# Half-precision pairs of the expert weights, split during projection and recurrent stage, and the experts' products as three passes

## What is computed

```python
def hier_moe(x, ...):                       # x: (tokens, 1024)
    grp  = argmax(xf @ router_coarse_w + b)          # 1 of 4 groups
    top_v, top_i = top_k(fine logits of that group, 2)   # 2 of 4 experts in it
    gate = softmax(top_v) * softmax(coarse)[grp]
    h = silu(xf @ expert_w1[e]) * (xf @ expert_w3[e])     # 1024 -> 256, 16 experts
    y = sum over the two experts of gate * (h @ expert_w2[e])   # 256 -> 1024
```

## Time and profile before

| | us |
|---|---|
| median of 3 runs | 1721.48 |
| profiled execution, its own time | 1725.69 |
| span of that execution, first to last instruction | 1724.1 |
| TensorE busy in the span | 1496.3 (87%) |
| VectorE, ScalarE, GpSimd busy | 796.5, 391.0, 358.0 |

### The profile page before, as it was taken

The page is one execution under the profiler, slowest core; times in us unless marked ns, Lnnn a source line. Parts: engine busy times, 40 slices in busy tenths (PEclk is TensorE's granted clock), DMA queues, the critical chain, the costliest instruction groups (busy, mean ns, idle before and its releaser), DMA issues. The chain is left out here.

```text
span 1724.1 us, 23759 instructions
## 1 busy us (share of the span) xinstructions
PE 1496.3 (87%) x8642; PEld 963.1 (56%) x8643; DVE 796.5 (46%) x1363; ACT 391.0 (23%) x689; POOL 358.0 (21%) x328
## 2 busy tenths in 40 slices
PE   6999999699898998998889399706999999995987
PEld 3555566388787787887776155503444444442443
DVE  5333111357766767677676644430111111124775
ACT  3001111123223222233221222101222222221332
POOL 0000000043352441533522111131000000002321
PEclk9999999899999999999988599857999999997999
DMA  9755442501012020120101522198577664314331
GB/s 390 264 203 184 178 149 112 206 1 66 13 66 80 1 78 29 51 78 13 36 13 57 199 110 109 55 356 320 206 301 294 249 233 176 109 67 150 131 126 54
DMA packets 60789, 237.74 MB, mean 138 GB/s; under 512 B 6672, under 2 KB 23696, under 8 KB 53912
## 3 DMA queue, kind: packets, MB, share of 16 engines
q1 hardware_dynamic: 37912, 152.30, 23.6%
q0 software_dynamic: 18176, 67.38, 10.5%
q10 hardware_dynamic: 4608, 16.78, 2.4%
HBM read 153.85 MB, written 82.61 MB: 137 GB/s over the span
## 5 line engine op out<-in xcount | busy, mean ns | idle before, releaser
L2065 PE MATMUL ex_ps<-ex_w,ex_xT 128*128 x512 | 227.3, 597 | 1.5 <-issue 1.5
L292 PE MATMUL pj_ps<-pj_wh,pj_xh 128*128 128x448 f16 (+1 forms) x576 | 196.1, 340 | 14.5 <-DVE pj_wl L181 14.5
L292 PE MATMUL pj_ps<-pj_wl,pj_xh 128*128 128x448 f16 (+1 forms) x576 | 196.2, 341 | 0.0
L292 PE MATMUL pj_ps<-pj_wh,pj_xl 128*128 128x448 f16 (+1 forms) x576 | 196.0, 340 | 0.0
L2065 PEld LDWEIGHTS ex_ps<-ex_w,ex_xT 128*128 128x128 f32 x512 | 95.6, 192 | 110.5 <-issue 110.5
L1491 POOL TENSOR_TENSOR mx_ET<-mx_G,arena 128x512 f32<-128x512 f32 x80 | 117.1, 1484 | 145.9 <-ACT mx_G L1040 136.5
L2168 DVE SCALAR_TENSOR_TENSOR ex_th<-ex_th,ex_ps 128x256 f32<-128x256 f32 x32 | 13.5, 421 | 233.1 <-ACT ex_th L2126 233.1
L2080 PE MATMUL ex_ps<-arena,ex_hidT 128*128 x256 | 115.3, 593 | 0.7 <-ACT ex_hidT L2130 0.7
L789 PE MATMUL mx_ps<-mx_M,mx_ET 128*128 128x128 f32 x672 | 94.1, 295 | 20.2 <-POOL mx_ET L1491 19.1
L804 PE MATMUL mx_ps<-mx_X,mx_MT 128*128 128x128 f32 x656 | 94.6, 290 | 11.3 <-ACT mx_X L1048 11.3
L789 PEld LDWEIGHTS mx_ps<-mx_M,mx_ET 128*128 128x128 f32 x672 | 85.2, 205 | 34.3 <-POOL mx_ET L1491 22.5
(11 more groups left out here) (415 smaller groups left out, 2593.0 us busy)
## 6 DMA issues: line engine op xcount, KB each, us to landing
ex_w<-in_w SPq DMA_DIRECT2D x16, 2048.0 KB, 9.0
sorted_h<-pj_zero POOLq DMA_DIRECT2D x32, 512.0 KB, 3.2
arena<-in_w SPq DMA_DIRECT2D x16, 1024.0 KB, 11.9
ex_x<-sorted_h POOLq DMA_DIRECT2D x32, 512.0 KB, 9.6
sorted_y<-ex_y ACTq DMA_DIRECT2D x32, 512.0 KB, 2.8
proj<-arena SPq DMA_DIRECT2D x72, 224.0 KB
pj_w<-in_w_mixed SPq DMA_DIRECT2D x4, 1792.0 KB, 14.0
mx_past<-proj SPq DMA_DIRECT2D x8, 896.0 KB, 6.6
```

Of the source, the lines that this page charges most:

```text
L292: mm = nc.tensor.matmul(bank[b][:, 0:width], x[:, m, k], packed(y, u, mixed)[:, k], start=(k == 0 and n == 0), stop=(k == KD - 1 and n == 2))
L2065: m = mm(B[u][:], xT[u][:, k], w13[:, slot, k].rearrange("p one f -> p (one f)"), start=(k == 0), stop=(k == KD - 1))
```

## The change

The experts' weights (16 x 3 MB) are handed to the program as 96 pieces of 128 x 1024 (`wx`), six per expert. Each piece is loaded, split into a high and a low half-precision part (scaled by 64, as in `project`), and written to a DRAM tensor `ws` in pairs. Pieces 0 to 60 are split in `project`, one per step from step 8 on, through a ring of four in the space of x (GpSimd issues load and store); pieces 61 to 95 in `mixer`, five per tile in tiles 0 to 6, through two slots in the space of `s0T` and `r0` (ScalarE issues load and store). So `s0T` and `r0` are loaded later, after the last pair is out. The zero fill moves from GpSimd in `project` to SP at the start of `mixer`, with rows of 1 KB. In `experts` the weights are loaded as pairs (the same bytes), x and the hidden rows are split after their transposes, and each product is three half-precision passes. The scales are taken back in the tanh, in the hidden split and in the routing weights.

```diff
@@ project: GpSimd, in place of the zero fill
+                def store(c):
+                    pool.wait_ge(pair_lo, c + 1)
+                    pool.dma_start(ws[c], pair[c % ring]).then_inc(pair_out[c % ring], 16)
+                pool.wait_ge(x_lo, 3)
+                for c in range(EARLY_CHUNKS):
+                    if c >= ring:
+                        pool.wait_ge(pair_out[c % ring], 16 * (c // ring))
+                    pool.dma_start(raw[c % ring], wx[c]).then_inc(raw_in[c % ring], 16)
+                    if c >= 2:
+                        store(c - 2)
...
@@ project: ScalarE and VectorE, at the end of each step
+                        act.wait_ge(raw_in[c % ring], 16 * (c // ring + 1))
+                        split_hi(nc.scalar, pair[c % ring][:, 0], raw[c % ring], W_SCALE).then_inc(pair_hi, 1)
...
+                        dve.wait_ge(pair_hi, c + 1)
+                        split_lo(nc.vector, pair[c % ring][:, 1], raw[c % ring], W_SCALE, pair[c % ring][:, 0]).then_inc(pair_lo, 1)
@@ mixer: SP
-            sp.dma_start(s0T[:], s0T_d).then_inc(s0T_in.sem, 16)
-            sp.dma_start(r0[:], r0_d).then_inc(s0T_in.sem, 16)
             load(1, 1, 0)
+            sp.wait_ge(half_set.sem, 3)
+            for j in range(SLOTS // P):
+                sp.dma_start(sorted_h.rearrange("(j p) (b c) -> j p b c", p=P, b=4)[j], zero[:].unsqueeze(1).broadcast_to([P, 4, 256])).then_inc(zeroed.sem, 16)
...
             load(NT, 0, NT // 2, sample=True)
+            for n in range(2):
+                sp.wait_ge(pair_out[n].sem, 16 * ((TILE_CHUNKS * (NT - 1) - n + 1) // 2))
+            sp.dma_start(s0T[:], s0T_d).then_inc(s0T_in.sem, 16)
+            sp.dma_start(r0[:], r0_d).then_inc(s0T_in.sem, 16)
             store(NT - 2)
@@ mixer: ScalarE
+            def put(t, u, m):
+                act.wait_ge(pair_d.sem, pair_d.at(t, m + 1))
+                at = (u + m) % 2
+                act.dma_start(ws[EARLY_CHUNKS + TILE_CHUNKS * t + m], pair[at]).then_inc(pair_out[at].sem, 16)
+            def chunk(t, u, i, m):
...
+                if m > 0:
+                    put(t, u, m - 1)
+                elif later(t, 1):
+                    put(t - 1, 1 - u, TILE_CHUNKS - 1)
+                if m < TILE_CHUNKS - 1:
+                    fetch(t, u, m + 1)
+                at, earlier = (u + m) % 2, TILE_CHUNKS * i + (TILE_CHUNKS * u + m) // 2
+                if later(t, 1) or m >= 2:
+                    act.wait_ge(pair_out[at].sem, 16 * earlier)
+                act.wait_ge(raw_in[at].sem, 16 * (earlier + 1))
+                split_hi(nc.scalar, pair[at][:, 0], raw[at], W_SCALE).then_inc(pair_a.sem, 1)
...
             def body(t, u, i):
                 turn(t)
+                first_fetch(t, u)
...
                 level(t, 1)
+                chunk(t, u, i, 0)
                 level(t, 2)
+                chunk(t, u, i, 1)
                 level(t, 3)
                 f_lora(t + 1, 1 - u)
                 f_kksq(t + 1)
+                chunk(t, u, i, 2)
                 level(t, 4)
                 f_loraT(t + 1)
                 f_z(t + 1, 1 - u)
+                chunk(t, u, i, 3)
                 level(t, 5)
...
                 eye(t + 1)
+                chunk(t, u, i, 4)
+                if isinstance(t, int) and t == NT - 1:
+                    put(NT - 2, 0, TILE_CHUNKS - 1)
@@ mixer: VectorE (the same five places: behind norms1, f_mix, norms2, norms3 and tail)
+                at = (u + m) % 2
+                dve.wait_ge(pair_a.sem, pair_a.at(t, m + 1))
+                split_lo(nc.vector, pair[at][:, 1], raw[at], W_SCALE, pair[at][:, 0]).then_inc(pair_d.sem, 1)
@@ experts: loads, up and down, splits
-        eng.dma_start(self.w13[:, u], self.w13_d[e]).then_inc(self.loaded[u].sem, 16)
+        eng.dma_start(self.w13[:, u], self.ws[e][:, 0:self.chunks13]).then_inc(self.loaded[u].sem, 16)
...
-                    pe.wait_ge(turn_a.sem, turn_a.at(j))
+                    pe.wait_ge(x_d.sem, x_d.at(j))
...
-                        m = mm(B[u][:], xT[u][:, k], w13[:, slot, k].rearrange("p one f -> p (one f)"), start=(k == 0), stop=(k == KD - 1))
+                        hi, lo = (w13[:, slot, k // 2, h, cols].rearrange("p one f -> p (one f)") for h in range(2))
+                        for n, (a, w) in enumerate(((xh, hi), (xh, lo), (xl, hi))):
+                            m = mm(B[u][:], a[u][:, k], w, start=(k == 0 and n == 0), stop=(k == KD - 1 and n == 2))
...
+                def turned(j, b):
+                    for half in range(2):
+                        dve.wait_ge(turn_a.sem, turn_a.at(j, half + 1))
...
+                        split_lo(nc.vector, xl[b % 2][:, r], B[2 + half][:].rearrange("p (k t) -> p k t", t=P), 1.0, xh[b % 2][:, r]).then_inc(x_d.sem, 1)
...
                 def step(j, b, i):
                     hidden(j, b)
+                    if not (isinstance(j, int) and j == NJ - 1):
+                        turned(j + 1, b + 1)
                     out(j - 1, b - 1, i)
+                    hid_turned(j, b)
```

More of the change, by code:

```diff
@@ L218, in project @@
         stored = [sem(f"stored{b}") for b in range(nb)]
-        zero = sb("zero", [P, D])
-        zero_set = sem("zero_set")
-        zeroed = soft.enter_context(nc.semaphore("pj_zeroed"))
+        room = xT[:].rearrange("p t k c -> p (t k c)")
+        ring = 4
+        raw = [room[:, 2 * CHUNK * u:2 * CHUNK * u + CHUNK] for u in range(ring)]
+        pair = [room[:, 2 * CHUNK * u + CHUNK:2 * CHUNK * (u + 1)].bitcast(F16).rearrange("p (h c) -> p h c", h=2) for u in range(ring)]
+        raw_in = [soft.enter_context(nc.semaphore(f"pj_raw_in{u}")) for u in range(ring)]
+        pair_out = [soft.enter_context(nc.semaphore(f"pj_pair_out{u}")) for u in range(ring)]
+        pair_hi, pair_lo = sem("pair_hi"), sem("pair_lo")
+        first_step = 2 * per * half - EARLY_CHUNKS - 3
+        assert first_step > 4
         def packed(w, u, mixed):
@@ L346, in _ @@
                         split_w_at(split_w, MIXED + 2 * i, q)
+                        pair_hi_at((half + i) * per + q)
             @block.vector
@@ L381, in _ @@
                         split_w_at(split_w, MIXED + 2 * i, q)
+                        pair_lo_at((half + i) * per + q)
 class Arena:
@@ L1450, in body @@
                 tail(t, u, mc)
+                chunk(t, u, 4)
             def end():
@@ L2078, in down @@
                         for f in range(NF):
-                            rows = w2[:, slot, f, 512 * half:512 * half + 512].rearrange("p one d -> p (one d)")
-                            m = mm(B[5 + half][:], hidT[u][:, f], rows, start=(f == 0), stop=(f == NF - 1))
+                            hi, lo = (w2[:, slot, f, h, 512 * half:512 * half + 512].rearrange("p one d -> p (one d)") for h in range(2))
+                            for n, (a, w) in enumerate(((hidh, hi), (hidh, lo), (hidl, hi))):
+                                m = mm(B[5 + half][:], a[u][:, f], w, start=(f == 0 and n == 0), stop=(f == NF - 1 and n == 2))
                         m.then_inc(down_p.sem, 1)
@@ L2085, in turn_hid @@
                     pe.wait_ge(hid_d.sem, hid_d.at(j))
+                    if not (isinstance(j, int) and j == 0):
+                        pe.wait_ge(hidl_d.sem, hidl_d.at(j - 1))
                     for f in range(NF):
```

112 lines of the change are left out of this document (84 added, 28 removed).

## The result

The changed kernel took **1694.35 us** (median of 4 runs, 1686.78 to 1696.48) against 1721.42 of the kernel before in the same session: a ratio of 0.9835, 95% interval 0.9803 to 0.9866. The forecast was 1700.5, with an own range of 1688 to 1715. The profiled execution has a span of 1693.5 us, 30.6 less than before; the forecast for it was 21 less.

What follows compares the result with a forecast made beforehand. TensorE bounds the experts, a chain across engines the recurrent stage. Experts -75, recurrent stage +53, rest +1, together -21 from 1725.7, then 4.2 lower for the median: 1700.5 us; own range 1688 to 1715, 8-in-10 range 1672 to 1727.

Steps and rivals of the forecast that it cites:

- Experts: Stage of the experts: three half-precision passes at 0.219 us replace each full-precision product, 2.40 us a tile; -75 us in all.
- the 2 put down for the start: First tiles of the experts: no down product lies between, so the split shows, about 2 us once.
- covered, but not by much: Experts 3 to 7: loads lag by 11 us, while the four-slot ring is 9 to 36 us ahead.
- Projection: Projection stage: 61 pieces hide beside a TensorE that is never idle; taken as 0, bound 8 us above.
- a sign of being wrong: Projection: ScalarE held at a piece by its load or by VectorE would show the forecast wrong; no size given.
- The chain through pieces 2 and 3: Recurrent tiles 0 to 6: these pieces delay the copies for levels 4 and 5; level 5 starts 4.6 us later a tile.
- VectorE beside GpSimd: Recurrent stage: piece 2's split reads two SBUF tensors, so waits for GpSimd's second mask; 2.4 us on VectorE, not 1.2.
- The masks of level 3: Recurrent stage: piece 0 on VectorE falls on GpSimd's two powers, whose end sets these masks; 0.7 us a tile.
- The clock: Recurrent stage: half-clock stretches behind the new TensorE waits in levels 4 and 5; 2.3 us a tile, bounds 0 and 5.8.
- Eats it all: Rival, recurrent stage: deep half-clock stretches and later masks make a tile cost 11.7 us; 1729.5 us, slower; chance 0.14.
- The pieces are cheap: Rival, recurrent stage: free register rows and no new half-clock stretch, 3.75 us a tile; 1673.5 us; chance 0.18.
- The experts give less: Rival, experts: 18 us loads empty the ring, or extra address rows cost TensorE; 10 to 20 us, about 1715; chance 0.10.

Runs made afterwards that it cites:

- two_passes: The changed kernel with the experts' products leaving out the pass on the weights' low halves, which are still loaded: 1667.95 us.
- filled_waits_half: The changed kernel with TensorE multiplying the identity, 7 products each ahead of its waits for the copies of levels 4 and 5: 1682.54 us.
- filled_waits: The changed kernel with TensorE multiplying the identity, 14 products each ahead of its waits for the copies of levels 4 and 5: 1686.48 us.
- later_and_filled: The changed kernel with pieces 2 and 3 placed later, and 7, 14 and 8 identity products at level 3's two masks and level 5's copies: 1659.73 us.

## Why the prediction was right

**Experts: right, one term a little small.** A pass was priced at 0.219, from 48 passes in 10.53 us; it is 0.216. That is 12 x 3 x 0.0036 = 0.13 us more a tile, 2.54 and not 2.40, 81.3 in all. From the first turn to the last product the stage took 371.6 us before and 292.5 now, 79.1 less; the 2.2 between this and 81.3 stand against the 2 put down for the start. The splits fit, and the two address rows per product show in no wait. The loads held too, although they came slower than forecast: from 1259 to 1426 us SP's issues were 12.2 to 17.7 us apart and not 13.0. The 3.19 MB a tile of the forecast stand on no row. That the loads were "covered, but not by much" is what two_passes shows.

**Projection: right within a microsecond or two.** TensorE has no gap. The last product starts at 321.18 (319.69 before), and at 319.6 to 321.0 in the twelve kernels of the experiments, which have the same projection; the first product of the next stage came 1 us later still, behind the loads that VectorE mixes. ScalarE waited 111 us for pieces there, at a DMA share of 0.96, and VectorE 82 us for ScalarE's halves. The forecast named the first of these as a sign of being wrong; it cost nothing, since TensorE waited for neither.

**Recurrent stage: the mechanism right but for one link, its two sizes off in opposite directions.** The forecast was 5.3 us a tile of waits and 2.3 of clock, 53 in all. Measured are 28.2 us of idle time, 4.0 a tile, and 19.8 of longer busy time, 2.8 a tile: 48. That the sum is nearer than its parts is luck.
- *The chain through pieces 2 and 3* was sized at +4.6 at the start of level 5. Counted from the turn ahead of level 4, that start is 3.8 to 5.2 later in the seven tiles, 4.4 on the mean; but part of that is already products at half clock. The waits alone grew by 1.8 (level 4) and 1.3 (level 5). What I overpriced is a piece on ScalarE: 2.1 us, but level 4 was held by 1.6 to 1.7 in five of the seven tiles. The larger part of the difference is the store's issue: it ran while ScalarE was still in the operation ahead (603.65 to 604.01, beside the square from 603.45 to 604.08, in the rows above), so that only one issue of 0.34 counts and not two.
- *VectorE beside GpSimd*: the forecast had piece 2 wait for the second mask; it took 2.29 in place of 1.22. Right in size, with a rule that was too narrow. The link behind it held in two tiles of seven only: by the forecast VectorE, late from this split, sets the decay's addition and by it the copies of level 5. In five tiles VectorE waited 0.38 to 0.63 us ahead of that addition for TensorE's product (the row of 613.70 above). These are the tiles where the first products behind level 4's wait ran at half clock; there the lateness came from ScalarE's piece by way of TensorE.
- *The masks of level 3*: 0.7 a tile forecast; the two waits together were 0.8 to 1.6 longer in five tiles of seven, 5.3 us in all, 0.75 a tile.
- *The clock*: 2.3 forecast, 2.8 measured; filled_waits_half showed that the waits bring it. Tile 7, which the forecast left as it was, has the waits of before and still takes 1.7 us more.

**The rivals.** "Eats it all" needed 10.7 us a tile: one interval of seven came near (75.0 in place of 64.6), the mean was 6.9. "The pieces are cheap" (3.75) fell by the waits and by the clock. "The experts give less" did not happen with three passes, and did, by the loads, with two.

Not settled: the 1 to 2 us by which merge, route and last stage were shorter; nothing in the change touches them, and no run tests it. The lengths of the stages rest on one profiled execution of each kernel; the experts, from the first turn to the last product, took 291.1 to 292.6 us in all twelve kernels with three passes.

## What to carry to other kernels

Work for an idle engine is free only if nothing that another engine already waits for is queued behind it: look for the places where the bound engine waits, keep them clear, and put the work behind what it waits for (here 42.7 us for moving two of five pieces by a few lines). A wait of TensorE can cost twice, in time and in the clock after it; a short filling that ends before the wait does gives the second part back, and one that is too long gives back less (filled_waits) or costs more than it saves (later_and_filled). Before counting on a product's price, count its records in the trace.
